# Encoder layer in one kernel: projection begun on two row tiles, its last block split by columns, transforms evicted first, and identity transposes placed around the first gather

## The reference

```python
h = rmsnorm(x, norm_mix)
u = h @ w_in                              # 1024 -> 2048
u_b, u_c, u_x, u_f = split(u)             # 512 columns each
v = u_c * u_x                             # short convolution, width 3, along the sequence
y_conv = rmsnorm(u_b * conv3(v, conv_w), g_conv)
y_four = rmsnorm(real(fft2(u_f in 8 groups of 64, axes=(seq, group))), g_fourier)
x = x + concat(y_conv, y_four) @ w_out
# expert choice, 16 experts, D_FF = 2816: each expert takes its top-k rows (128 prompt, 32 sample)
xt = rmsnorm(x, norm_ffn)
aff = softmax(xt @ w_router)
gates, idx = top_k(aff.T, cap)
ye = (silu(xt[idx] @ w_gate) * (xt[idx] @ w_up)) @ w_down * gates
out = rmsnorm(x + scatter_add(ye, idx), norm_final)
```

## Time and profile before

| | |
|---|---|
| time, median of 3 runs | 2585.72 us (2581.74 to 2586.13) |
| the profiled execution | 2586.17 us, of which its span is 2584.3 us |
| PE busy | 2449.8 us (95%) |
| PEld, DVE, ACT, POOL busy | 1917.9, 1638.5, 1346.8, 155.9 us |
| mean granted clock of TensorE | 0.974 |
| HBM | 242 GB/s over the span |
| chain that ended last | PE 90%, DVE 4%, issue 3%, ACT 2%, DMA 1% |

### The profile page before, as it was taken

How to read it: one execution, slowest core, us unless ns; L and a number is a source line. 1 busy time by engine, 2 the same in 40 slices (tenths; PEclk the granted TensorE clock), 3 DMA queues, 4 the chain that set the end, 5 groups by cost and what they waited for, 6 DMA issues and landing times.

```text
span 2584.3 us, 44975 instructions
## 1 busy us (share of the span) xinstructions
PE 2449.8 (95%) x18271; PEld 1917.9 (74%) x18271; DVE 1638.5 (63%) x1367; ACT 1346.8 (52%) x1243; POOL 155.9 (6%) x207
## 2 busy tenths in 40 slices
PE   6999999299999999999999999999999999999997
PEld 5888788277777777777777777777777777777775
DVE  4433448766666666767576757675767576757575
ACT  5322223255555565656565656565656565655565
POOL 0021000000100000000001000000010101000101
PEclk8999999599999999999999999999999999999998
DMA  5102142447878787878777877778787868686877
GB/s 188 33 17 74 52 162 106 157 174 278 307 276 286 274 287 274 298 269 303 269 293 269 297 274 284 277 281 290 268 293 266 304 254 307 252 319 240 321 271 279
DMA packets 295967, 628.13 MB, mean 243 GB/s; under 512 B 21360, under 2 KB 72688, under 8 KB 295536
## 3 DMA queue, kind: packets, MB, share of 16 engines
q1 hardware_dynamic: 284160, 587.87, 62.1%
q0 software_dynamic: 11632, 37.51, 4.9%
HBM read 599.10 MB, written 26.21 MB: 242 GB/s over the span
## 4 chain that ended last, share of the span: by engine, by line
PE 90%; DVE 4%; issue 3%; ACT 2%; DMA 1%; POOL 0%; SPq 0%; POOLq 0%; DVEq 0%; ACTq 0%
PE ps L378 21%; PE ps L379 20%; PE ps L380 20%; PE ps L1508 12%; PE ps L1297 8%; PE ps L1516 6%; PE ps L1526 1%; DVE i L1050 1%; DVE v L1048 1%; DVE A L1052 1%; ACT win_h L626 1%; PE ps L1467 1%; DVE win_l L891 1%; DMA raw<-in_w_down_dram 0%; PE ps L1535 0%
## 5 line engine op out<-in xcount | busy, mean ns | idle before, releaser
L1180 DVE TENSOR_TENSOR spl_l<-raw,spl_h 128x2048 fp32r<-128x2048 f32 x528 | 1208.6, 2292 | 577.7 <-ACT spl_h L782 560.5
L782 ACT ACTIVATE spl_h<-raw 128x2048 fp32r<-128x2048 f32 x528 | 1011.8, 1917 | 569.9 <-PE ps L380 520.0
L379 PE MATMUL ps<-spl_l,xT 128*128 128x512 f32 x1408 | 556.6, 395 | 31.5 <-issue 31.5
L378 PE MATMUL ps<-spl_h,xT 128*128 128x512 f32 x1408 | 560.7, 398 | 6.0 <-issue 3.5
L380 PE MATMUL ps<-spl_h,xT 128*128 128x512 f32 x1408 | 554.1, 394 | 0.0
L379 PEld LDWEIGHTS ps<-spl_l,xT 128*128 128x128 f32 x1408 | 268.2, 190 | 91.1 <-issue 37.0
L378 PEld LDWEIGHTS ps<-spl_h,xT 128*128 128x128 f32 x1408 | 267.8, 190 | 82.8 <-issue 26.2
L1508 PE MATMUL ps<-raw,xTs 128*32 128x256 f32 (+1 forms) x6144 | 314.2, 362 | 0.0
L380 PEld LDWEIGHTS ps<-spl_h,xT 128*128 128x128 f32 x1408 | 268.1, 190 | 57.1
L378 PE MATMUL ps<-spl_h,g 128*128 128x512 f32 x704 | 278.3, 395 | 2.4 <-DVE spl_l L1180 2.4
L379 PE MATMUL ps<-spl_l,g 128*128 128x512 f32 x704 | 274.5, 390 | 0.0
(11 more groups left out here) (229 smaller groups left out, 1904.6 us busy)
## 6 DMA issues: line engine op xcount, KB each, us to landing
raw<-in_w_up_dram SPq DMA_DIRECT2D x352, 512.0 KB, 7.8
raw<-in_w_gate_dram SPq DMA_DIRECT2D x352, 512.0 KB, 8.7
raw<-in_w_down_dram SPq DMA_DIRECT2D x176, 1024.0 KB, 13.9
win_raw<-in_w_in_dram SPq DMA_DIRECT2D x16, 512.0 KB, 3.9
xt<-in_x_dram SPq DMA_DIRECT2D x10, 512.0 KB, 8.8
xr<-in_x_dram SPq DMA_DIRECT2D x10, 512.0 KB, 4.1
acc_dram<-xr SPq DMA_DIRECT2D x10, 512.0 KB, 2.6
xn_dram<-xn SPq DMA_DIRECT2D x10, 512.0 KB, 2.8
```

The source lines that it names most:

```text
L378: eng.matmul(o, a_h, b_h, start=first, stop=False, skip_group_check=True)
L379: eng.matmul(o, a_h, b_l, start=False, stop=False, skip_group_check=True)
L782: act.activation(spl_h[:, i % SPL, :], raw[:, slot_of(i), :], ACT.Copy).then_inc(sh_ok, 1)
L1180: dve.tensor_tensor(spl_l[:, i % SPL, :], raw[:, slot_of(i), :], spl_h[:, i % SPL, :].bitcast(F32), ALU.subtract).then_inc(sl_ok, 1)
```

## The change

- The root table of ScalarE is loaded by a dummy `Sqrt` of one element before the first row tile arrives. Row tiles 0 and 1 are loaded ahead of `gmix`; the load of `dd` on GpSimd's queue moves behind the wait for seven scaled row tiles.
- TensorE transposes two row tiles instead of four, then runs block 0 on rows 0 to 256, then on rows 256 to 512. The other transposes move to other steps k. Blocks 0 and 1 swap their last pieces: the rows 1024 to 1280 of block 0 come ahead of the rows 512 to 1024 of block 1. `square_x`, `scale_x`, `win_hi` and `win_lo` are reordered to match.
- `waves(j, 0)` on VectorE stands ahead of `win_lo(n + 1)`; `waves(j, 1)` and the sample's stay behind it (and behind `taps`).
- Block 15 is done as rows 0 to 512, then rows 512 to 1280, each raising `u_done`. `conv_out(3)` and the staging of row tile 0 follow the first piece. `ysh`, `ysl` and `wof_raw` get other places in SBUF so that this is allowed, and the first two pieces of `wof_raw` are loaded earlier.
- 48 transposes of the identity into bank 0 stand between the list transposes and `gathered(1)`, and 24 between `gathered(1)` and `expert(0)`.

```diff
-        wof_raw = at("wof_raw", 40 * KB, [P, JH, D])
+        wof_raw = [at(f"wof_raw{k}", o * KB, [P, D]) for k, o in enumerate((148, 156, 48, 52))]
-        ysh = at("ysh", 16 * KB, [P, 2, KD, P], F32R)
-        ysl = at("ysl", 24 * KB, [P, 2, KD, P], F32R)
+        ysh = [at(f"ysh{n}", o * KB, [P, KD, P], F32R) for n, o in enumerate((140, 20))]
+        ysl = [at(f"ysl{n}", o * KB, [P, KD, P], F32R) for n, o in enumerate((144, 28))]
...
+            for t in range(2):
+                sp.dma_start(xt[:, t, :], x_t[t]).then_inc(x_in[t], 16)
             sp.dma_start(gmix[:, :], norm_mix[0].rearrange("(k p) -> p k", p=P), allow_slow_non_contiguous=True).then_inc(gmix_in, 16)
-            sp.dma_start(xt[:, 0, :], x_t[0]).then_inc(x_in[0], 16)
             load_win(0)
-            for t in range(1, 5):
+            for t in range(2, 5):
...
-            sp.wait_ge(hT_half, 1)
+            sp.wait_ge(u_done, PROJ - 1)
+            sp.wait_ge(winl_ok, PROJ)
             for k in range(JH):
-                sp.dma_start(wof_raw[:, k, :], wout_v[JH + k]).then_inc(wof_in[k // 2], 16)
+                if k == 2:
+                    sp.wait_ge(hT_half, 1)
+                sp.dma_start(wof_raw[k][:, :], wout_v[JH + k]).then_inc(wof_in[k // 2], 16)
...
-            act.wait_ge(ident_ok, 4)
+            act.wait_ge(ident_ok, 3)
+            act.activation(rt2[:, 0:1], eps[:, 0:1], ACT.Sqrt)
...
             for t in range(TILES):
-                if t + 2 < TILES:
-                    square_x(t + 2)
+                if t == 2:
+                    square_x(2)
+                    square_x(3)
+                    win_hi(1)
+                if 3 <= t < TILES - 1:
+                    square_x(t + 1)
                 act.wait_ge(xT_ps, t + 1)
...
+            scale_x(1)
+            win_lo(0)
             for t in range(TILES):
-                if t + 1 < TILES:
-                    scale_x(t + 1)
-                if t == 1:
-                    win_lo(0)
...
+                if t == 1:
+                    scale_x(2)
+                    scale_x(3)
+                if t == 3:
+                    scale_x(4)
                     win_lo(1)
+                if 3 <= t < TILES - 2:
+                    scale_x(t + 2)
...
-                    conv_out(j)
+                    conv_out(j, 0, T)
+                if 3 <= n < 3 + JH:
+                    waves(n - 3, 0)
                 if n + 1 < PROJ:
                     win_lo(n + 1)
...
                 if 3 <= n < 3 + JH:
-                    waves(n - 3)
+                    waves(n - 3, 1)
+                    short_waves(n - 3)
...
-            conv_out(JH - 1)
+            conv_out(JH - 1, 0, 512)
...
             stage_lo(0, 0)
-            for k in range(JH, KD):
-                wo_lo(k)
+            wo_lo(JH)
+            wo_lo(JH + 1)
+            conv_out(JH - 1, 512, T)
+            wo_lo(JH + 2)
+            wo_lo(JH + 3)
...
-            for t in range(4):
+            for t in range(2):
                 turn_x(t)
...
+            pe.wait_ge(hTl_ok, 2)
+            project(0, 0, 256, more_x({1: 2, 4: 3}))
             pe.wait_ge(hTl_ok, 4)
-            project(0, 0, 512, more_x({1: 4, 4: 5}))
+            project(0, 256, 512, more_x({4: 4}))
             pe.wait_ge(winl_ok, 2)
-            project(1, 0, 512, more_x({1: 6, 4: 7, 7: 8}))
+            project(1, 0, 512, more_x({0: 5, 3: 6, 6: 7}))
             pe.wait_ge(hTl_ok, 8)
-            project(0, 512, 1024, more_x({2: 9}))
-            pe.wait_ge(hTl_ok, 9)
-            project(1, 512, 1024)
+            project(0, 512, 1024, more_x({0: 8, 3: 9}))
             pe.wait_ge(hTl_ok, TILES)
             project(0, 1024, T)
+            project(1, 512, 1024)
             project(1, 1024, T)
...
-                project(n, 0, T, posts(n))
+                if n < PROJ - 1:
+                    project(n, 0, T, posts(n))
+                else:
+                    project(n, 0, 512)
+                    project(n, 512, T)
...
+            def idle_turns(count):
+                for _ in range(count):
+                    pe.transpose(bank(0)[:, 0:P], ident[:, :], ident[:, :])
...
+            idle_turns(48)
             gathered(1)
+            idle_turns(24)
             expert(0, False)
```

More of the change, by code:

```diff
@@ L434, in load_unit @@
                     sp.dma_start(dst, src).then_inc(raw_in[slot_of(i)], 16)
-            sp.wait_ge(u_done, PROJ)
+            sp.wait_ge(u_done, PROJ + 1)
             sp.dma_start(gffn[:, :], norm_ffn.partition_broadcast(P)[:, 0, :]).then_inc(gffn_in, 16)
@@ L637, in _ @@
                                bank((4, 6)[t % 2], 2).rearrange("p (k t) -> p k t", k=KD), ACT.Copy).then_inc(hTh_ok, 1)
-                if t == 4:
-                    win_hi(1)
             def halves(j):
@@ L688, in conv_square @@
             def conv_square(j):
-                act.wait_ge(y_ok, j + 1)
+                act.wait_ge(y_ok, j + 1 + (j == JH - 1))
                 act.activation((sqc if j else qc)[:, :], yconv[:, j, :], ACT.Square).then_inc(sqc_ok, 1)
@@ L697, in wo_hi @@
                     act.wait_ge(wof_in[(n - JH) // 2], 32)
-                    act.activation(wof_h[:, n - JH, :], wof_raw[:, n - JH, :], ACT.Copy,
+                    act.wait_ge(hT_half, 1)
+                    act.activation(wof_h[:, n - JH, :], wof_raw[n - JH][:, :], ACT.Copy,
                                    scale=gm2[:, n:n + 1]).then_inc(woh_ok, 1)
@@ L730, in stage_hi @@
                         act.wait_ge((y_ok, yf_ok)[h], (JH, 8 * JH)[h])
-                    act.activation(ysh[:, s, JH * h:JH * (h + 1), :], y[:, :, bass.ds(t * P, P)], ACT.Copy).then_inc(ysh_ok, 1)
+                    act.activation(ysh[s][:, JH * h:JH * (h + 1), :], y[:, :, bass.ds(t * P, P)], ACT.Copy).then_inc(ysh_ok, 1)
             def group_exp(n):
@@ L928, in channels_lo, with waves, short_waves @@
                                       Y_h[:, 2 * p:2 * p + 2, :].bitcast(F32), ALU.subtract).then_inc(Yl_ok, 1)
-            def waves(j):
-                yp, ysm = yfour[:, j, 0:SEQ], yfour[:, j, SEQ:T]
+            def waves(j, i):
+                yp = yfour[:, j, 0:SEQ]
                 b = bank(6)
[L933 to L938, removed]
+                up_, down_, o, w, r0, r1 = (
+                    (yp[:, 0:SEQ // 2 + 1:2], yp[:, SEQ - 2:SEQ // 2:-2], 0, SEQ // 4 + 1, 1, SEQ // 4),
+                    (yp[:, 1:SEQ // 2:2], yp[:, SEQ - 1:SEQ // 2:-2], HE, SEQ // 4, 0, SEQ // 4))[i]
+                dve.wait_ge(qcp_ok, 4 * j + i + 1)
+                dve.tensor_tensor(up_, b[:, 0:w], qcp[:, o:o + w], ALU.subtract).then_inc(yf_ok, 1)
+                dve.tensor_tensor(down_, b[:, r0:r1], qcp[:, o + r0:o + r1], ALU.add).then_inc(yf_ok, 1)
+            def short_waves(j):
+                ysm = yfour[:, j, SEQ:T]
+                b = bank(6)
                 dve.wait_ge(qcp_ok, 4 * j + 4)
@@ L969, in taps, with conv_out @@
                     dve.wait_ge(ty_ok, j * 2 + i)
-            def conv_out(j):
+            def conv_out(j, t0, t1):
                 n = JH + 3 * j + 2
                 u = bank(3 * (n % 2), 3)
-                dve.wait_ge(u_done, n + 1)
+                dve.wait_ge(u_done, n + 1 + (t0 > 0))
                 if j == 0:
                     dve.wait_ge(ds_done, 3 * JH)
-                dve.tensor_tensor(yconv[:, j, 0:SEQ], u[:, 0:SEQ], tc[:, 0:SEQ], ALU.mult)
-                dve.tensor_tensor(yconv[:, j, SEQ:T], u[:, SEQ:T], tc[:, SEQ + 2:T + 2], ALU.mult).then_inc(y_ok, 1)
+                mid = min(t1, SEQ)
+                last = dve.tensor_tensor(yconv[:, j, t0:mid], u[:, t0:mid], tc[:, t0:mid], ALU.mult)
+                if t1 > SEQ:
+                    last = dve.tensor_tensor(yconv[:, j, SEQ:T], u[:, SEQ:T], tc[:, SEQ + 2:T + 2], ALU.mult)
+                last.then_inc(y_ok, 1)
             def wo_lo(n):
@@ L982, in wo_lo @@
                 k = n % JH
-                full, hi, lo = ((woc_raw, woc_h, woc_l) if n < JH else (wof_raw, wof_h, wof_l))
-                dve.scalar_tensor_tensor(out=lo[:, k, :], in0=full[:, k, :], scalar=gm2[:, n:n + 1],
+                full, hi, lo = ((woc_raw[:, k, :], woc_h, woc_l) if n < JH else (wof_raw[k][:, :], wof_h, wof_l))
+                dve.scalar_tensor_tensor(out=lo[:, k, :], in0=full, scalar=gm2[:, n:n + 1],
                                          in1=hi[:, k, :].bitcast(F32), op0=ALU.mult, op1=ALU.subtract).then_inc(wol_ok, 1)
@@ L1016, in stage_lo @@
                     hs = slice(JH * h, JH * (h + 1))
-                    dve.tensor_tensor(ysl[:, s, hs, :], y[:, :, bass.ds(t * P, P)], ysh[:, s, hs, :].bitcast(F32),
+                    dve.tensor_tensor(ysl[s][:, hs, :], y[:, :, bass.ds(t * P, P)], ysh[s][:, hs, :].bitcast(F32),
                                       ALU.subtract).then_inc(ysl_ok, 1)
@@ L1298, in project @@
                                              start=(k == 0 and i == 0), stop=(k == KD - 1 and i == 2), skip_group_check=True)
```

(7 more changed lines are left out.)

3 lines of the change are left out of this document (1 added, 2 removed).

## The result

The changed kernel takes 2507.97 us (median; 2507.4 to 2508.75), the kernel before beside it 2585.93 us (2581.74 to 2587.72): a ratio of 0.9701 [0.9684, 0.9718], 78 us faster. I had forecast 24.6 us faster, 2561 us, and the range ended at 2554. The sign came out, and each of the four priced parts came within 1 us by the traces; the forecast misses 53 us that come from a place which I had set aside in its first paragraph.

A forecast was written before the change was run, and what follows sets the result against it. PE bounds the kernel, busy 95% of the span, so its stalls and half-clock stretches count. 10.3 + 7.1 + 6.2 + 1.0 = 24.6 us off 2586.17 is 2561.6, forecast as 2561; range 2554 to 2571.

The forecast's parts named there:

- four priced parts: Savings up to expert 0: the start 10.3 us, transforms first 7.1, last block by columns 6.2, identity transposes 1.0.
- The step that failed: First paragraph: the expert loop's return, PE's largest wait group, 31.5 us in 13 times, is not touched by the diff.
- rival 4: Expert loop's return: 72 added instructions cause a second 2.4 us fetch stop per pass, 34 us, giving 2595; chance 0.04.
- the check I had set: All of the difference, about 25 us, stands before expert 0; an expert loop pass of another length means wrong.
- Rival 2: Expert loop: an earlier start shifts clock drops at the returns; a drop every pass costs 12 us, 2573; chance 0.12.
- the start: Table load, row tiles, blocks 0 and 1: block 2 starts near 56.1 instead of 64.81; 10.3 us saved.
- transforms first: `waves(j, 0)` ahead of `win_lo`, blocks 3 to 6, removes most `yfour` waits: 7.1 us saved, bounds 5.5 and 8.3.
- last block: Block 15 by columns: PE goes on without its 3.89 us wait, warm; 6.2 us saved, bounds 3.9 and 6.7.
- rival 5: No net change: the saving before 400 us is lost to VectorE's top-k already running on its own; chance 0.02.
- rival 3: Front falls short: late `gmix` or a missed wait, 6 us less, 2567; chance 0.14 together with Rival 1.
- The identity transposes: 48 and 24 around the first gather warm the clock for expert 0: 1.0 us saved, between -4 and +2.7.
- Rival 1: Identity transposes around the first gather stay cold: 19.6 us saved instead of 24.6, 2566; chance 0.14 together with rival 3.

The follow-up runs named there:

- run 7: Kernel before plus 96 identity transposes (192 PE instructions) in the wait for the lists: 2535.11 us, ratio 0.9805.
- Runs 2 and 7: Kernel before plus 128 identity transposes in the wait for the lists: 2585.65 us; the same with 96: 2535.11 us.
- Runs 9 to 11: Kernel before, padded to place +192, with one edit each: the start 2524.25 us; transforms ahead of `win_lo` 2526.32 us; block 15 in two pieces 2527.06 us.
- run 3: Changed kernel without its 72 identity transposes around the gather: 2577.45 us, ratio 0.9968 against the kernel before.
- run 6: Changed kernel with its 72 identity transposes moved from around the gather into the wait for the lists: 2509.7 us, ratio 0.9706 against the kernel before.
- the run of 2778.55 us: A fourth run of the kernel before with only block 15 in two pieces and 96 pad transposes, left out: 2778.55 us at mean granted clock 0.841.

## Why the prediction was off by 53 us

**The step that failed** is the one in the first paragraph: the return of the loop, "31.5 us in 13 times, which the diff does not touch". The diff does not touch the loop's code; it touches its address. I took a wait for `issue` as a fixed property of the branch. The same step is in rival 4, which names the right mechanism ("it must fetch its instructions again", 72 transposes "just ahead of that code") but sees it as able only to add a stop, at 0.04, and never as able to remove one. It counts 72 instructions, where the traces have 144 for the transposes and 193 for the whole diff. And it prices the stop without the clock: the stops' 31.5 + 3.5 us are less than the 50.7 that run 7 gives back. By the pass: 127.1 us with a stop alone, 128.7 with a drop of the clock behind it, 124.39 with neither. So of the remaining 15.7 us some 11 are the clock (7 drops of 1.6 us), and some 4 are what such a pass grows beyond its stop of 2.42 us (0.3 us, 13 times); what these are is not shown.

**The forecast of all the difference ahead of expert 0** was the check I had set ("a pass of the expert loop of another length" would be wrong), and it is what fails: 24.6 us stand there and 52.9 behind it.

**Rival 2** had the second half of it. It put the idle 2.4 us at the end of a pass, where the trace has them 20 instructions into the next, and it saw that the clock drops hang on the loop's return, but tied them to the time at which the loop starts. Runs 2 and 7 begin expert 0 at 519.14 and 519.15 us and take 2585.7 and 2535.1 us: it is the place and not the phase.

**The front terms were nearly right.** The traces of before and after give each of them at a point where one part of the change ends:

| first matmul of | before | after | earlier by | this part | forecast |
|---|---|---|---|---|---|
| block 3 (the start) | 84.01 | 73.70 | 10.3 | 10.3 | 10.3 |
| block 7 (transforms first) | 187.90 | 169.57 | 18.3 | 8.0 | 7.1 |
| the norm sums (last block) | 330.80 | 305.53 | 25.3 | 6.9 | 6.2 |

The lists come 25.2 us earlier, against a sum of 23.6. Single steps hold to a few tenths: block 0 at 15.36 (15.2), the swap that frees block 2 (56.12 against 56.1), the wait for `hT_l` 1.68 (1.8), for `yfour` 0.92 (1.2). VectorE's top-k moved forward with the row tiles, so rival 5 did not occur, and no wait that I had missed came up (rival 3). Of the 0.9 us that the transforms give beyond the forecast, 0.8 stand in blocks 3 to 5: they are 4.7 us shorter together, where I had counted the 3.9 us of their waits alone. The last block gives 0.2 us more than its upper bound of 6.7. Runs 9 to 11, with 10.9, 8.8 and 8.1 us by the medians and 11.2, 9.0 and 5.8 by the start of expert 0, confirm that each edit works by itself, but they size it only to within the drops and the shift of the kernel before named above; they do not show that the transforms went past their bound of 8.3. The lower bound of the transforms, 5.5, was added up wrongly: with a third of the 3.9 us gone it is 5.8.

**The identity transposes** gave 0.9 us by the traces and 1.7 by the medians, forecast 1.0. The mechanism was the one priced between its bounds: the 48 raise the clock, the clock falls again in the wait for the gather, the 24 run partly cold and delay expert 0 a little, which then starts warm. Rival 1, that transposes keep the clock down, is refuted by the 48 themselves. Its price of -4 us was wrong as well: it counts the cold start of expert 0 as a loss, which is in the kernel before too, and without it the sum is -2.7. What made them look worth 70 us (run 3 against the changed kernel) is that they are 144 instructions.

**Adding up**: 50.7 (place, run 7) + 10.9 + 8.8 + 8.1 (runs 9 to 11) + 1.7 (run 6) = 80.2 by medians, 78.0 measured; the 2.2 us between them are within the blur of runs 9 to 11.

**Open**: the edges of the good stretch between 96 and 144 and between 224 and 256; why the loop's exit costs 3.4 to 3.7 us at 0, 256 and 257 and nothing at 32, 49 and 96; what part `hint_back_edge` has in it; and whether the run of 2778.55 us has any cause in the kernel.

## What to carry to other kernels

In a kernel like this, where an engine's program has a loop of 2059 instructions, an edit anywhere ahead of it also moves the loop's code. Read the waits for `issue` at the loop's return in both profiles before crediting an edit, and compare variants at the same place (here: the same count of that engine's instructions ahead of the loop, modulo 256), with a pad in a wait that is there anyway. Taking an edit out by itself is not a clean test when it changes that count: run 3 would have given the transposes 70 us, where they are worth one or two us. And where such stops are in a profile, idle instructions ahead of the loop are the cheapest thing to try, with several counts: here 96 transposes brought 50.7 us in 2586, and 16 cost 32.

## What the runs showed of the hardware

- Instructions arrive in transfers of 16 KB (160 of them, 2.62 MB, before). The return of this loop costs PE between nothing and 4.51 us by the place of the loop's head (the table above), with one period of 256 instructions measured as equal: 2585.65 against 2585.84 us.
- A stop of PE of 2.4 us can bring the granted clock down to half behind it, in 7 of 13 passes before: the pass is then 128.7 us long instead of 127.1. With stops of 3.79 us (run 3) it fell behind all 13.
- Transposes alone raise the granted clock: it went from half to full 5.9 us into the row of 48.
